# Attention steps that take two query heads of both key heads, with scores on alternating row halves and values on two column halves

## What is computed

```
s = einsum('bnqhgd,bnjhd->bnhgqj', qb, kb) * HEAD_DIM ** -0.5
s = where(valid, s, -1e30)
m = maximum(max(s, -1), sk)
e = exp(s - m)
p = e / (sum(e, -1) + exp(sk - m))
o = einsum('bnhgqj,bnjhd->bnqhgd', p, vb)
```

## Time and profile before

| | |
|---|---|
| median of 3 runs | 1254.37 us (1252.78 to 1256.11) |
| profiled execution | 1254.12 us, its span 1252.4 us |
| granted TensorE clock, mean | 0.979 |
| PE busy | 1199.0 us (96%) |
| PEld busy | 1093.6 us (87%) |
| DVE busy | 697.6 us (56%) |
| ACT busy | 368.3 us (29%) |

### The profile page before, as it was taken

How to read it: one execution, slowest core, us unless ns; L and a number is a source line. 1 busy time by engine, 2 the same in 40 slices (tenths; PEclk the granted TensorE clock), 3 DMA queues, 4 the chain that set the end, 5 groups by cost and what they waited for, 6 DMA issues and landing times.

```text
span 1252.4 us, 17266 instructions
## 1 busy us (share of the span) xinstructions
PE 1199.0 (96%) x6524; PEld 1093.6 (87%) x6524; DVE 697.6 (56%) x1150; ACT 368.3 (29%) x554; POOL 79.1 (6%) x112
## 2 busy tenths in 40 slices
PE   6989999999999999999998799999999999999995
PEld 1576678788899999999888799999999999999885
DVE  3876877887446565455545577553355433233434
ACT  3631114443541121132224522113311231123314
POOL 1101110000111111100000000000000000000001
PEclk7989999999999999999999899999999999999998
DMA  8733453231142232265322243331133112121212
GB/s 305 309 126 111 153 190 118 102 101 51 47 144 93 93 110 102 96 241 163 107 87 85 91 137 128 131 134 66 52 117 117 67 51 67 67 68 52 84 33 101
DMA packets 42592, 140.77 MB, mean 112 GB/s; under 512 B 4603, under 2 KB 10315, under 8 KB 41516
## 3 DMA queue, kind: packets, MB, share of 16 engines
q1 hardware_dynamic: 26256, 83.19, 19.3%
q0 software_dynamic: 11232, 44.05, 10.0%
q10 hardware_dynamic: 5052, 12.81, 2.9%
HBM read 124.30 MB, written 15.74 MB: 112 GB/s over the span
## 4 chain that ended last, share of the span: by engine, by line
PE 83%; DVE 8%; issue 3%; DMA 3%; ACT 2%; SPq 0%; DVEq 0%; ACTq 0%
PE acc_ps L560 59%; PE acc_ps L630 9%; PE wk L851 3%; PE wk L677 2%; PE wk L791 2%; PE wk L771 2%; PE wk L829 2%; DMA mod_raw<-in_w_ada_rows 1%; PE acc_ps L637 1%; PE wk L781 1%; PE wk L670 1%; DVE hy_cross L1613 1%; DVE dot_out L1412 1%; DVE w_lo L1316 1%; DMA hy_spec<-spec 1%
## 5 line engine op out<-in xcount | busy, mean ns | idle before, releaser
L560 PE MATMUL acc_ps<-act_hilo,w_hi 128*128 128x384 f32 x2304 | 511.6, 343 | 9.9 <-DVE act_hilo L1365 4.0
L560 PEld LDWEIGHTS acc_ps<-act_hilo,w_hi 128*128 128x128 f32 x2304 | 411.4, 190 | 31.9 <-issue 24.8
L560 PE MATMUL acc_ps<-act_hilo,w_lo 128*128 128x384 f32 x1152 | 294.9, 337 | 0.0
L1001 ACT ACTIVATE w_hi<-w_raw 128x1024 fp32r<-128x1024 f32 x108 | 114.4, 1059 | 335.7 <-PE acc_ps L560 310.8
L560 PEld LDWEIGHTS acc_ps<-act_hilo,w_lo 128*128 128x128 f32 x1152 | 210.0, 189 | 0.0
L1316 DVE TENSOR_TENSOR w_lo<-w_raw,w_hi 128x1024 fp32r<-128x1024 f32 x108 | 131.9, 1221 | 75.4 <-ACT w_hi L1001 75.2
L560 PE MATMUL acc_ps<-hidden_hilo,w_hi 128*128 128x384 f32 x768 | 164.1, 334 | 0.0
L560 PEld LDWEIGHTS acc_ps<-hidden_hilo,w_hi 128*128 128x128 f32 x768 | 135.9, 188 | 0.0
L1783 DVE TENSOR_TENSOR n_h<-ev_tmp 128x768 f32<-128x768 f32 x32 | 30.7, 958 | 145.6 <-ACT ev_tmp L1276 145.6
L560 PE MATMUL acc_ps<-hidden_hilo,w_lo 128*128 128x384 f32 x384 | 97.5, 334 | 0.0
L1723 DVE SCALAR_TENSOR_TENSOR xT<-acc_ps,modT,xT 128x384 f32 (+2 forms) x72 | 30.4, 479 | 91.0 <-PE acc_ps L560 91.0
(11 more groups left out here) (204 smaller groups left out, 1293.6 us busy)
## 6 DMA issues: line engine op xcount, KB each, us to landing
w_raw<-in_w_pre SPq DMA_DIRECT2D x54, 512.0 KB, 3.3
dot_ring<-in_w_ada_cols POOLq DMA_DIRECT2D x52, 512.0 KB, 3.6
w_raw<-in_w_up SPq DMA_DIRECT2D x32, 512.0 KB, 3.3
w_raw<-in_w_down SPq DMA_DIRECT2D x32, 512.0 KB, 3.3
mod_raw<-in_w_ada_rows SPq DMA_DIRECT2D x12, 512.0 KB, 8.8
spec<-filt_out POOLq DMA_DIRECT2D x12, 512.0 KB, 3.1
gate_spill<-gates_out ACTq DMA_DIRECT2D x16, 384.0 KB, 2.3
hy_spec<-spec SPq DMA_DIRECT2D x12, 512.0 KB, 5.6
```

Source lines behind the costliest of these rows:

```text
L560: mm = pe.matmul(acc_ps[:, slot, 512 * h:512 * h + HALF], w[:, kw, :], src[:, x, k, HALF * h:HALF * h + HALF], start=(first and i == 0), s ...
L1001: act_e.activation(whi[s][:] if to is None else to[0], raw[s][:], ACT.Copy).then_inc(hi_done, 1)
```

## The change

A step takes a query block and a pair of j (`jh`), that is query heads 2jh and 2jh+1 of both key heads, in place of one key head with its four query heads. The four scores matmuls keep their shapes, but go through the row halves 0, 64, 0, 64 in turn. The matmul of `values` on a block of keys becomes two: 64 weight columns (v of one key head) and 256 moving columns each, one to output partitions 0 to 63, one to 64 to 127, in the same bank. `values_out` copies 128 x 256. The sink logits are reordered on the host. Shapes and counts of `turned`, of the softmax and of all waits stay.

```
--- before.py
+++ after.py
@@ -58,7 +58,8 @@
 
 UNITS = ((0, 0, 2), (0, 2, 2), (1, 0, 4))
 STEPS = [(u, r) for r in range(2) for u in range(3)]
-ATT = [(qb, kv) for qb in range(NTB) for kv in range(2)]
+ATT = [(qb, jh) for qb in range(NTB) for jh in range(2)]
+ATT_ROWS = (0, 2, 1, 3)
 
 
 MODS = ((SH1, 0), (SC1, 0), (SH1, 4))
@@ -763,11 +764,12 @@
 
             def scores(n):
 
-                qb, kv = ATT[n]
+                qb, jh = ATT[n]
                 first, nk, _ = att_keys(qb)
-                h = slice(HD * kv, HD * kv + HD)
-                for j in range(NJ):
-                    c = take("scores", n, j)
+                for i, r in enumerate(ATT_ROWS):
+                    kv, j = r // 2, 2 * jh + r % 2
+                    h = slice(HD * kv, HD * kv + HD)
+                    c = take("scores", n, i)
                     pe.matmul(wk[:, c:c + P * nk], qk[h, j, P * qb:P * qb + P], qk[h, 4, P * first:P * (first + nk)],
                               start=True, stop=True).then_inc(s_ready, 1)
 
@@ -788,8 +790,9 @@
                 c = take("values", n, 0)
                 for kb in range(nk):
                     pe.wait_ge(p_copied, done + kb + 1)
-                    mm = pe.matmul(wk[:, c:c + 512], V[:, first + kb, :], PT[:, n % 2, kb, :],
-                                   start=(kb == 0), stop=(kb == nk - 1))
+                    for kv in range(2):
+                        mm = pe.matmul(wk[HD * kv:HD * kv + HD, c:c + 256], V[:, first + kb, HD * kv:HD * kv + HD],
+                                       PT[:, n % 2, kb, 256 * kv:256 * kv + 256], start=(kb == 0), stop=(kb == nk - 1))
                 mm.then_inc(o_ready, 1)
 
             def turn(n):
@@ -1138,11 +1141,10 @@
                     act_e.activation(PT[:, n % 2, kb, :], wk[:, c:c + 512], ACT.Copy).then_inc(p_copied, 1)
 
             def values_out(n):
-                qb, kv = ATT[n]
-                h = slice(HD * kv, HD * kv + HD)
+                qb, jh = ATT[n]
                 act_e.wait_ge(o_ready, n + 1)
                 c = bank("values", n, 0)
-                act_e.activation(qk[h, 0:NJ, P * qb:P * qb + P], wk[h, c:c + 512].rearrange("p (j n) -> p j n", j=NJ),
+                act_e.activation(qk[:, 2 * jh:2 * jh + 2, P * qb:P * qb + P], wk[:, c:c + 256].rearrange("p (j n) -> p j n", j=2),
                                  ACT.Copy).then_inc(o_copied, 1)
 
             def turn_out(n):
@@ -1569,20 +1571,20 @@
 
             def softmax_in(n):
 
-                qb, kv = ATT[n]
+                qb, jh = ATT[n]
                 _, nk, m0 = att_keys(qb)
                 b = n % 2
                 if n >= 2:
                     dve.wait_ge(p_ready, sum(att_keys(q)[1] for q, _ in ATT[:n - 1]))
-                for j in range(NJ):
-                    c = bank("scores", n, j)
-                    dve.wait_ge(s_ready, NJ * n + j + 1)
+                for i, j in enumerate(ATT_ROWS):
+                    c = bank("scores", n, i)
+                    dve.wait_ge(s_ready, NJ * n + i + 1)
                     dve.tensor_tensor_reduce(S[:, b, j, 0:P * nk], wk[:, c:c + P * nk], mask[:, m0:m0 + P * nk],
-                                             HD ** -0.5, sink[:, NJ * kv + j:NJ * kv + j + 1], ALU.add, ALU.max,
+                                             HD ** -0.5, sink[:, NJ * jh + j:NJ * jh + j + 1], ALU.add, ALU.max,
                                              mx[:, b, j:j + 1]).then_inc(s_max, 1)
                 dve.wait_ge(s_max, NJ * n + NJ)
                 dve.tensor_scalar(nmx[:, b], mx[:, b], -1.0, None, ALU.mult).then_inc(s_neg, 1)
-                dve.tensor_tensor(sd[:, b], sink[:, NJ * kv:NJ * kv + NJ], mx[:, b], ALU.subtract).then_inc(s_sd, 1)
+                dve.tensor_tensor(sd[:, b], sink[:, NJ * jh:NJ * jh + NJ], mx[:, b], ALU.subtract).then_inc(s_sd, 1)
 
             def softmax_out(n):
                 b = n % 2
@@ -1914,6 +1916,7 @@
         return np.concatenate([np.asarray(r).reshape(-1, P) for r in rows], axis=0).T
 
     h = {n: np.asarray(inputs[n]) for n in _RAW}
+    h["attn_sink"] = h["attn_sink"].reshape(2, 2, 2).transpose(1, 0, 2).reshape(h["attn_sink"].shape)
     x = np.concatenate([np.asarray(inputs["x_sample"])[0], np.asarray(inputs["x_prompt"])[0]], axis=0)
     h["x_T"] = x.T.reshape(KD, P, T).transpose(1, 0, 2)
     c = np.stack([np.asarray(inputs["c_sample"])[0].reshape(KD, P), np.asarray(inputs["c_prompt"])[0].reshape(KD, P)])
```

## The result

The changed kernel takes 1241.99 us (median of 6 runs, 1239.28 to 1244.47) against 1253.9 us before (6 runs, 1249.01 to 1256.11): 11.9 us less, ratio 0.9907 with a 95% interval of 0.9889 to 0.9924. Two later comparisons of the same kernel gave 0.9936 (0.9912 to 0.9960) and 0.9895 (0.9876 to 0.9914). The forecast was 1246.6 us in a range of 1242 to 1258: right in its sign, but with 7.5 us for a saving of 11.9, so that the result lies at the lower edge of the range. What came was the rival to which I had given 0.08, whole doubling, at 1242.6.

The account below looks back on a forecast made before the run. PE was taken to bound attention. Values 5.95 or 3.6 us, scores 2.75 or 2.6, end 0.1, together 8.8 or 6.3; middle 7.5: 1254.1 - 7.5 = 1246.6 us, 8-in-10 range 1242 to 1258.

Parts of the forecast that it names:

- whole doubling: Rival, chance 0.08: passes pair up completely, 4 or 6 places for values, 4 for scores; 11.5 us saved, 1242.6 us.
- PE bounds attention; time taken from it counts: Attention, 200 to 359 us: chain is PE end to end, so time taken from PE counts until another engine is late.
- only a2 runs with b1: Scores: last pass of one matmul overlaps first pass of the next, on the other row half; 5 places instead of 8.
- 5 places or 7: Values with two or three key blocks: 8 or 12 passes take 5 places (1.08 us) or 7 (1.51 us).
- The rival's terms: Whole doubling, chance 0.08, values: 0.86-0.35 us saved with two key blocks, 1.29-0.35 with three.
- Whether the load of the other half stands in the open: Each new half might wait for its weight load: 0.11 us at b1 in scores, half of 0.11 in values.
- my bound: From whole overlap to load in the open: values and scores save 8.8 or 6.3 us together with the end.
- Two new changes of shape cost 0.35 us a step: Values: full-width weights to half costs 0.15 us in, 0.20 us out, 0.35 us together.
- ACT's copies keep most of the scores' gain: Third and fourth scores wait for banks ACT empties; 0.65 us saved in three three-block stages, 0.05 in two-and-two stages.
- The bank of values, held by DVE's read: Values wait for DVE's read of the first scores; in four two-block stages scores saved there are worth nothing.
- DVE's chain of 14.2 us is the wall of three-block stages: With four dot products, last scaling ends at g+14.2 (g: end of tile's last matmul); room 0.77 us, loss 0.3 once.
- The end: Last values lead over ACT's copy to the spectra load; their saving counts, and ACT's smaller copy gives about 0.1 us.

Follow-up runs that it names:

- e_cols_grouped: Changed kernel with values run for all key blocks of one column half first, then for the other; 1240.45 us (4 runs).
- e_scores_part: Only the scores' part of the change, values as in the kernel before; 1248.81 us (10 runs) against 1252.2 before, ratio 0.9973.
- e_dots_spread: Changed kernel with one dot product less in each of the four stages that have two, four of them later; 1239.18 us, ratio 0.9901 to before.
- e_after: The changed kernel itself, run again beside e_scores_part and e_cols_grouped; 1241.95 us (4 runs) against 1252.2 before.
- e_copies_first: Changed kernel with ACT's copies of the transposed blocks ahead of its convolution step instead of behind; 1269.82 us (4 runs), ratio to before 1.0131.

## Why the prediction was right or wrong

- *PE bounds attention; time taken from it counts.* Right: 11.1 us left the chain between the end of tile 8 and the inverse transform.
- *The two passes of one matmul share a half, so only a2 runs with b1.* Wrong, and the step that cost the forecast. I let only neighbouring passes in program order overlap. But the first of the other half starts with the first of this one, past the second: each half works through its own passes, and all of them pair up. The term "5 places or 7" should have been 4 and 6; values save 0.86 and 1.29 us before the shape change, not 0.48 to 0.64 and 0.79 to 1.07. By stages, two blocks: before 1.73 + 6.25 us for values and six k-steps, after 1.01 + 6.44: 0.53. Three blocks: 2.58 + 6.25 against 1.45 + 6.47: 0.91. The rival's terms were 0.51 and 0.94.
- *Whether the load of the other half stands in the open.* Neither end of my bound came: loads of both halves come together (eight in 0.63 us above). The Trainium skill's rule that a weight load overlaps only where row groups differ (TensorE: Matmul & The Clock Gate, "Packing small matmuls — row/col tiling") is not what these column halves show, which share all their rows. The same section says that matmuls start strictly in program order; in e_cols_grouped the third starts with the first and before the second. The measurement decides. The Trainium skill's up to 2x for half-size operands (TensorEngine Tiling, "Theoretical Speedup") did hold for the passes of values: eight of them in four places.
- *Two new changes of shape cost 0.35 us a step.* Right: k-steps behind values take 0.2 us more, and in the way in the load stands 0.05 us in the open after about 0.1 without work.
- *ACT's copies keep most of the scores' gain.* Right, and to the size where DVE doesn't delay the transposes: in the three-block stage at 223 us scores end 3.38 us after the tile's end instead of 4.01 (0.63; I had 0.65), in a two-block one at 291 us 2.68 instead of 2.72 (0.04; I had 0.05), at 201 us 0.44 (0.33 to 0.48). ACT's row in the chain after, and e_scores_part's 2.8 us, say the same.
- *The bank of values, held by DVE's read.* Right; eight waits instead of four, where I said about six, but each (0.30 us on average) hardly longer than the 0.27 us for which the load of values stands still without it.
- *DVE's chain of 14.2 us is the wall of three-block stages.* Right, shown by e_dots_spread. With the larger saving it was met four times instead of once or twice: PE needs 13.67, the stages take 14.03 and 14.07. It took 0.36 to 0.40 us from each of three stages, 1.1 us in all, where the sum had 0.3 once: late transposes do hold the next tile. Here the forecast had luck. The three-block stages of about 14.0 us that it named came true (14.03 and 14.07), but out of a larger saving on PE and a larger loss to DVE.
- *The end.* The last values' saving counted, about 1.1 us with what followed instead of 0.4. Half of it is PE's own (0.72 less for values, 0.19 more behind them). The other half is a wait that was there before and that the forecast left out: the inverse transform stood behind DVE's products, which need the spectra load. After, it doesn't wait (in e_after 0.18 us).

```profile
381.06 1.13 PE L851 MATMUL wk<-dft_inv,hy_prod 128*128 128x256 f32 x4 [0.57 <-DVE hy_prod L1617]
```

## What to carry to other kernels

When float32 matmuls are put on halves of the array in turn, don't pair up only neighbouring passes: here each half worked through its own, and values on two halves with half the columns cost half, 0.86 us instead of 1.72, before the change of shape. Don't let more than two matmuls of one half stand ahead of the other's. Then look at once for who frees the banks and what each engine does in a stage, since these walls took back most of the scores' gain here. A step moved ahead of another on one engine can close a loop through a third: before moving it, follow what starts the next stage's longest chain. And where PE then stands still, look at the granted clock too.

## What the runs showed that I hadn't expected

- Two halves run in lockstep with matmuls that are two apart in the program. The second half joins as soon as no more than two matmuls of the first are unfinished: at once with two, after one with three matmuls of 256 columns (0.49 us with the load), after two with four of 128 columns (0.49), after four with six (0.93).
- All this is for float32 matmuls with two passes each, and for column halves, which read the same 128 partitions. That two matmuls start together is seen for row halves too (211.19 above); how far ahead that reaches isn't shown there, since the third scores wait for ACT's copies.
- DVE's scaling took 3.11 us instead of 1.14 with POOL's fold beside it, in all three runs in which the fold fell on it. Nothing was run to test the cause.
- In e_copies_first the granted clock fell to about half for some 3 us in four stages, each time behind a wait of PE of 1.9 us, though not behind every such wait. A two-block stage with a fall took 1.5 us more.
